# Slabs of seven products: every weight tile at byte 192, every combination of x at byte 0, and two unread matmuls at the head of each stretch

## What is computed

```python
# first block
h = h + 0.5 * swiglu(rms_norm(h, g1), w1, w3, w2)          # feed-forward, width 2816
u = rms_norm(h, g2); proj = u @ w_in                       # q, k, v, pool, gates
h = h + (gates0 * (attn @ w_ba) + gates1 * (pool @ w_bp)) @ w_out
h = rms_norm(h + 0.5 * swiglu(rms_norm(h, g3), ...), g4)   # second feed-forward
# second block
q, k, v, g = split(rms_norm(h) @ ret_w_in); h = h + rms_norm((norm(retention(q, k, v)) * silu(g)) @ ret_w_out)
kv = rms_norm(h) @ w_kv; q, g = split(rms_norm(h) @ sb_w_in)
h = h + rms_norm((stick_breaking_attention(q, k, v) * silu(g)) @ sb_w_out)
```

## The kernel before

| product | a11 | s3 | s2 | a12 | s1 | a22 | s4 |
|---|---|---|---|---|---|---|---|
| stationary weights at byte | 192 | 0 | 0 | 192 | 0 | 192 | 192 |
| moving x at byte | 0 | 192 | 192 | 0 | 192 | 0 | 0 |

## Time and profile before

### The profile page before, as it was taken

How to read it: one execution, slowest core, us unless ns; L and a number is a source line. 1 busy time by engine, 2 the same in 40 slices (tenths; PEclk the granted TensorE clock), 3 DMA queues, 4 the chain that set the end, 5 groups by cost and what they waited for, 6 DMA issues and landing times.

```text
span 1843.8 us, 28142 instructions
## 1 busy us (share of the span) xinstructions
PE 1828.2 (99%) x11305; PEld 1636.9 (89%) x11311; DVE 1396.5 (76%) x1912; ACT 930.0 (50%) x1274; POOL 81.5 (4%) x109
## 2 busy tenths in 40 slices
PE   9999999999999999999999999999999999999997
PEld 7998998888889988988998899988888888888886
DVE  8875887888778889866888987776777776666566
ACT  6652664435355536633653555455547644444445
POOL 0000000020001000000000000000000000000000
PEclk9999999999999999999999999999999999999999
DMA  6744763462407535743752678632231222222213
GB/s 215 181 120 133 199 161 116 164 158 77 114 26 210 155 114 149 188 149 110 191 146 95 199 211 240 231 137 77 107 137 61 79 92 69 92 81 79 91 68 92
DMA packets 60595, 244.78 MB, mean 133 GB/s; under 512 B 6865, under 2 KB 9457, under 8 KB 49857
## 3 DMA queue, kind: packets, MB, share of 16 engines
q1 hardware_dynamic: 46016, 199.25, 32.3%
q0 software_dynamic: 14032, 43.38, 12.3%
q10 hardware_dynamic: 432, 0.56, 0.1%
HBM read 223.76 MB, written 13.11 MB: 128 GB/s over the span
## 4 chain that ended last, share of the span: by engine, by line
PE 72%; DVE 5%; ACT 2%; issue 1%; DMA 0%; DVEq 0%; POOL 0%; ACTq 0%
PE acc L2570 14%; PE acc L2571 13%; PE acc L2572 13%; PE acc L2577 6%; PE acc L2576 6%; PE acc L2578 6%; PE att L2571 2%; PE att L2572 2%; PE att L2570 2%; PE att L2576 1%; PE att L2578 1%; PE att L2577 1%; DVE w_lo L1454 1%; PE acc L2838 1%; PE acc L2813 1%
## 5 line engine op out<-in xcount | busy, mean ns | idle before, releaser
L1454 DVE TENSOR_TENSOR w_lo<-raw,w_hi 128x2048 fp32r<-128x2048 f32 (+1 forms) x106 | 238.9, 2254 | 48.7 <-ACT w_hi L736 48.4
L736 ACT ACTIVATE w_hi<-raw 128x2048 fp32r<-128x2048 f32 (+1 forms) x106 | 199.3, 1880 | 75.3 <-PE acc L2572 61.9
L2570 PE MATMUL acc<-x_hi,w_hi 128*128 128x512 f32 x488 | 193.3, 396 | 0.9 <-DVE x_lo L1517 0.6
L2576 PE MATMUL acc<-xt_hi,w_hi 128*128 128x256 f32 x684 | 191.6, 280 | 0.0
L2578 PE MATMUL acc<-xt_hi,w_lo 128*128 128x256 f32 x684 | 191.3, 280 | 0.0
L2577 PE MATMUL acc<-xt_lo,w_hi 128*128 128x256 f32 x684 | 191.3, 280 | 0.0
L2572 PE MATMUL acc<-x_hi,w_lo 128*128 128x512 f32 x488 | 190.3, 390 | 0.0
L2571 PE MATMUL acc<-x_lo,w_hi 128*128 128x512 f32 x488 | 190.1, 390 | 0.0
L835 ACT ACTIVATE tmp<-acc 128x256 f32<-128x256 f32 x228 | 86.8, 380 | 124.6 <-PE acc L2578 114.8
L2571 PE MATMUL acc<-g_lo,w_hi 128*128 128x512 f32 x352 | 137.0, 389 | 0.0
L2570 PE MATMUL acc<-g_hi,w_hi 128*128 128x512 f32 x352 | 137.0, 389 | 0.0
(11 more groups left out here) (510 smaller groups left out, 5116.0 us busy)
## 6 DMA issues: line engine op xcount, KB each, us to landing
raw<-in_ffn_down SPq DMA_DIRECT2D x32, 704.0 KB, 4.0
raw_c<-in_ffn_seven SPq DMA_DIRECT2D x37, 512.0 KB, 5.3
raw<-in_ffn_seven SPq DMA_DIRECT2D x33, 512.0 KB, 4.9
raw<-in_ffn_seven POOLq DMA_DIRECT2D x33, 512.0 KB, 7.4
raw<-in_ffn_seven SPq DMA_DIRECT2D x37, 256.0 KB, 4.6
raw<-in_ret_values SPq DMA_DIRECT2D x8, 1024.0 KB, 4.7
raw<-in_ret_out SPq DMA_DIRECT2D x8, 1024.0 KB, 6.8
raw<-in_sb_v SPq DMA_DIRECT2D x8, 1024.0 KB, 4.8
```

The source lines that it names most:

```text
L736: nc.scalar.activation(w_hi[:, slot, at:at + cols], raw[:, slot, 0:cols], ACT.Copy).then_inc(w_hi_ready, 1)
L1454: tt(w_lo[:, slot, at:at + cols], raw[:, slot, 0:cols], w_hi[:, slot, at:at + cols].bitcast(F32), ALU.subtract).then_inc(w_ready, 1)
L2570: mm(dst, still[0], move[0], start=first, stop=False)
L2576: mm(dst, still[0], move[0], start=first, stop=False, skip_group_check=True)
```

## The change

The free columns in a slot of the split weights move: 48 of them (byte 192) now stand before the first quarter, and the four quarters follow each other without a gap, so all four begin at byte 192. The filler before `xt_hi` loses 192 bytes and the one behind `xt_lo` gains them, so that the combinations of x begin at byte 0 and all that follows stays where it was. With that all seven products have stationary weights at 192 and moving x at 0. Besides, in the first slab of each stretch (`opens`), one more matmul is put in the middle of the first product (a11) and one in the middle of the second (s3), behind their first six matmuls. Its stationary operand is a block of `x_hi` (byte 0), its moving one 256 columns of the slot's weights (byte 192), the opposite places of all its neighbours. It writes to the unused `LATE` columns of the same bank, which nobody reads.

```diff
+UNREAD = 1
-W_SUMMED = slice(2 * QUART + 64, SLAB + 64)
+LATER_LINE = LINE * 3 // 4
+W_SUMMED = slice(LATER_LINE + 2 * QUART, LATER_LINE + SLAB)
@@ def lone
-            return v[:, slot, 0:2 * (QUART + LINE * 3 // 4)].rearrange("p (k q) -> p k q", k=2)[:, :, 0:QUART]
+            return v[:, slot, LATER_LINE:LATER_LINE + 2 * QUART].rearrange("p (k q) -> p k q", k=2)
@@ tiles
-            sb("to_line_4", [P, 48 + 3 * DC * P], F32, scope)
+            sb("to_line_4", [P, 3 * DC * P], F32, scope)
             xt_hi = sb("xt_hi", [P, 3, TB, TOK // 2], F32R, scope)
             xt_lo = sb("xt_lo", [P, 3, TB, TOK // 2], F32R, scope)
-            sb("to_line_5", [P, 16], F32, scope)
+            sb("to_line_5", [P, LINE], F32, scope)
@@ TensorE
-            def product(dst, still, move, first, done=seg_done):
+            def product(dst, still, move, first, done=seg_done, between=None):
                 for c in range(TB):
+                    if between and c == TB // 2:
+                        between()
+            def unread(dst, slot):
+                for _ in range(UNREAD):
+                    mm(dst[:, LATE], x_hi[:, 0, 0:P], w_hi[:, slot, LATER_LINE:LATER_LINE + TOK // 2], start=False, stop=False, skip_group_check=True)
@@ seven
-                                   (0, QUART + LINE * 3 // 4, 2 * QUART + LINE, 3 * QUART + LINE))
+                                   (LATER_LINE + QUART * k for k in range(PARTS)))
-                product(two[:, EARLY], a11, b11, True)
+                product(two[:, EARLY], a11, b11, True, between=opens and partial(unread, two, slot))
-                product(one[:, EARLY], s3, t3, True)
+                product(one[:, EARLY], s3, t3, True, between=opens and partial(unread, one, slot))
@@ callers: opens=i == 0 (feed-forwards, retention), opens=k == 0 (mix)
```

More of the change, by code:

```diff
@@ L13 @@
 import numpy as np
+from functools import partial
 import concourse.bass as bass
@@ L2656, in product, with seven @@
                 ins.then_inc(done, 1)
-            def seven(first, side=None, fourth=(x_hi[:, 0:TB, LATE], x_lo[:, 0:TB, LATE])):
+            def unread(dst, slot):
+                for _ in range(UNREAD):
+                    mm(dst[:, LATE], x_hi[:, 0, 0:P], w_hi[:, slot, LATER_LINE:LATER_LINE + TOK // 2], start=False, stop=False, skip_group_check=True)
+            def seven(first, side=None, fourth=(x_hi[:, 0:TB, LATE], x_lo[:, 0:TB, LATE]), opens=False):
                 pe.wait_ge(w_ready, n.at(RING + 1))
@@ L2702, in ffn @@
                     for i in range(HALF if half else HALF - full):
-                        seven(forms if half == i == 0 else None)
+                        seven(forms if half == i == 0 else None, opens=i == 0)
                     op.next(HALF)
@@ L2932, in _ @@
                 for k in range(2):
-                    seven(6 if j == 1 and k == 0 else None, side)
+                    seven(6 if j == 1 and k == 0 else None, side, opens=k == 0)
             at = op.k
@@ L3058, in _ @@
             for i in range(RET_SEVEN):
-                seven(12 if i == 0 else None, fourth=(t4_hi, t4_lo))
+                seven(12 if i == 0 else None, fourth=(t4_hi, t4_lo), opens=i == 0)
                 if i == TURN_AFTER:
```

## The result

The changed kernel takes 1858.74 us, the median of four runs (1857.72 to 1859.12), against 1846.93 us for the kernel before beside it: a ratio of 1.0064, with a 95% interval of 1.0051 to 1.0076. It is slower by 0.64%; the forecast was 1839.0 us, within 1836.5 to 1850.0. The first rival had 1860.0 us.

The account below looks back on a forecast made before the run. TensorE was taken to bound the kernel. 49 slabs saving 0.18 us each (8.82) less 8 first slabs losing 0.09 (0.72) give 8.1 us off 1847.12: 1839.0 us, range 1836.5 to 1850.0, chance 0.58.

Parts of the forecast that it names:

- first rival: Single unread matmuls are not whole entries, so every stretch stays at the long pace to its end; 1860.0 us, chance 0.22.
- What bounds the kernel: TensorE fills the eight stretches of slabs, 554.02 us; a nanosecond saved per matmul there comes off the end.
- Two paces: In a stretch's middle slabs, matmuls follow each other every 113 or 118 ns, depending on what went before.
- three standings: In stretches: opening long, second long, short; x going from byte 0 to 192 moves on one, short back to second long.
- Part 1: All seven products at the same places: a slab of 9.52 us if short (0.18 saved), 9.90 if long (0.20 lost).
- Part 2: Two unread matmuls per first slab turn the stretch short from mid s3; 120 ns each, 0.09 us lost, eight times.
- the stuck case: The outcome of the first rival: stretches stay long to their end, 1860.0 us, chance 0.22.
- No new wait is due: Beside TensorE in a stretch: VectorE needs 90.65 us of what would be 105 us, so a quicker TensorE is covered.

Follow-up runs that it names:

- three in a row: The changed kernel with three unread matmuls in a row at each place (a11 and s3) instead of one: 1845.57 us, 0.9997 of the kernel before.
- a single group: The changed kernel with three unread matmuls in the middle of a11 alone, none in s3: 1862.47 us.
- the version with two and three: Changed kernel, two then three unread matmuls in a11, none in the mix, second head in the retention, ScalarE's copy before its split in last feed-forward slabs: 1843.62 us.
- the run with two: The changed kernel with two unread matmuls in a row at each place instead of one: 1860.73 us, 1.0076 of the kernel before.
- with five: The changed kernel with five unread matmuls in a row at each place instead of one: 1847.23 us.
- those with twelve: The changed kernel with twelve unread matmuls in a row at each place instead of one: 1863.13 us.
- both groups in a11: The changed kernel with two groups of three unread matmuls, both in a11 (behind its third and ninth matmul), none in s3: 1846.75 us.

## Why the prediction was wrong

- **What bounds the kernel: right.** What the stretches lost came onto the end: 12.1 us in the stretches, 11.8 in the medians.
- **Two paces, three standings: right.** The paces are 1.36 and 1.41 us per product with the new places too (short with three in a row, long in the changed kernel); within a run at the same places the pace stayed through 14 slabs, the four transposes included; and two entries, with the second long standing between them, lead from the opening to the short pace. The run with three in a row at both places shows this in all eight stretches, and the one with a single group that the first entry alone changes no pace. What the prediction lacked is that a stall turns the pace as well, with no change of place: the hiccup that it names in the last slab of the retention is one.
- **Part 1: right, size and sign.** All products at the same places keep the pace with which a stretch opens. "Without the second part this would be a loss": the places alone cost 0.53%.
- **Part 2 is the step that failed:** "Each is an entry and a return, in small." The trace of before had entries of 12 and 24 matmuls, and I carried them over to one. One moves nothing: with the old places the single one in a11 left the pattern of the kernel before as it was. In the changed kernel the second met the same standing as the first and did nothing either. So the term of the sum that failed is the whole saving: 49 slabs at 9.89 us in place of 9.52. The price of an unread matmul (120 ns taken, 115 measured) was not at fault.
- **The first rival was right in the outcome and half right in the reason.** Its sum, 1860.0 us, missed by 1.3 us; all eight heads went one way, and it decided at the third product, as said. Its reason, that one matmul has no pairing of a load from byte 0 with a stream from 192, is not what decides: four and seven have such pairings and move nothing. That the turn to short takes three matmuls would explain why two in the second group failed; three, five and twelve there fit it, but nothing else shows it.
- **The weights given:** 0.58 for the forecast against 0.22 was too much on one side for a step for which no row of the trace had an example. The range ended below the stuck case and so could not hold it.
- **"No new wait is due": wrong for a short stretch.** VectorE's total has room, but ScalarE's order in the last slab and the retention's transfers do not. The changed kernel didn't meet this, since it never became short; had it done so, the saving would have been some 3 us less than forecast; that is an estimate from the run with three in a row (1.4 us in place of 4.3).

## What to carry to other kernels

Where the same matmul shows two paces in a trace, read start to start through the boundaries and write down what turns the pace and what keeps it, before changing places: an arrangement that never turns the pace also keeps the wrong one. A repair that is a shortened form of something seen in the trace (one matmul for twelve) is a new thing, to be tried by itself at several lengths. And a stretch that gets two per cent quicker meets waits that had 0.1 or 0.2 us to spare; those within a stretch here also threw the pace back.

## What the runs showed of the hardware that I had not expected

- With 128x128 weights and 256 moving float32r columns at the full clock, matmuls follow each other every 113.3 or every 117.8 ns, over hundreds of them, with operands and places unchanged. Which of the two it is depends on what ran before.
- At the pace that opens a stretch, a run of matmuls at opposite places changes what follows or not by its number modulo three: 1, 4, 7 and 25 do not, 2, 3, 5, 12 and 24 do. In the long pace the gaps themselves repeat every three (on average 117.4, 117.6 and 118.3 ns), with high, low and high operands as well as in a group of twelve equal unread ones. Three gaps are 353.3 ns, 848 cycles of the 2.4 GHz that were granted, which three does not divide; that the rule of three comes from there is argued, not shown.
- A stall of 0.05 to 0.8 us can turn the pace either way: short to long at s1 in five stretches of the run with three and, with the smallest stall, in the retention of the version with two and three; long to short in one stretch of the run with two. It need not: 0.6 us in one step of the mix, in the run without unread matmuls, left the pace long. The same four transposes left it short in the runs with three and with five and made it long in those with twelve and with both groups in a11. What decides there stays open, as does the place in the chip where loads and streams meet, and whether it is the byte of the weights or that of x that counts.
